# Fewer modulation sums in attention, more in the first feed-forward layer: a two-layer decoder trunk in fp32

## The chip, the cores and the metric

The kernel runs on one core of one Trainium2 chip. The metric is the device time of one execution in microseconds, as the median of the runs shown. Rows of the trace come from one profiled execution.

## The reference

`x` is (1, 256, 1024), all in fp32. Two layers; the first mixes by dilated attention, the second by a gated recurrence, and each is followed by a SwiGLU layer. What matters here is the modulation and the normalisation of q and k:

```python
c_act = jax.nn.silu(c)
for i in range(DEPTH):
    mod = c_act @ ada_w[i] + ada_b[i]          # ada_w[i]: 1024 x 6144
    sh1, sc1, g1, sh2, sc2, g2 = jnp.split(mod[:, None, :], 6, axis=-1)
    h = rms_norm(x, norm_mix[i]) * (1.0 + sc1) + sh1
    ...  # y = dilated_attention(h, ...) or hgrn2_mixer(h, ...)
    x = x + g1 * y
    h = rms_norm(x, norm_ffn[i]) * (1.0 + sc2) + sh2
    x = x + g2 * swiglu(h, ffn_w1[i], ffn_w3[i], ffn_w2[i])

# in dilated_attention, for each of three head groups g (8 heads of 128)
q = rms_norm(qkv[:, :, g, 0], q_gain[g])
k = rms_norm(qkv[:, :, g, 1], k_gain[g])
v = qkv[:, :, g, 2]
```

## The kernel before

**Units.** All weight matrices pass through the core in 126 units of 128 x 2048 numbers. A unit is loaded by a DMA (`raw`), rounded to fp32r by ScalarE (`round_unit`, `whi`), its rest is formed by VectorE (`split_unit`, `wlo`, L1388), and TensorE multiplies high by high, low by high and high by low (L516, 24 products of 512 columns, or 48 of 256). ScalarE and VectorE work two units ahead: in their step m they round and split unit m + 2, and beside it they do what follows from TensorE's unit m. Units 0 to 35 are the q, k, v products of attention, in four pairs of heads with nine units each (`pr, j = divmod(m, 9)`); 36 to 39 are its output product; then come 33 units of the feed-forward layer 0 (`M_FFN0` = 40; unit r of the layer is unit 40 + r, and "unit 18 of the layer" below is r = 18). In the middle of that layer the units repeat in threes: two of them form a block of gate and up products (kinds 0 and 1), the third (kind 2) is a product with w2. After kind 1 ScalarE takes the silu (L1228), VectorE multiplies (L1726), TensorE transposes (L855), and the result is rounded and split (L1718).

**Attention beside the units.** A chunk of q and k (256 x 512) is squared by ScalarE (`qk_square`), reduced by VectorE (`qk_reduce`, L1614), ScalarE takes the root (`qk_rsqrt`, L1012 and L1014), and VectorE refines it and scales the chunk (`qk_normalise`, L1483 to L1488 and two of L1627). TensorE transposes the scaled chunk (`qk_transposes`, L697) behind the next unit. In the pairs from the second on, the reduction lies in steps with j = 1, 3, 5, the normalisation in those with j = 2, 4, 6, and the transposes behind unit j = 3 to 8. There the heads of the pair before are also attended: in even steps TensorE does scores (L716) and values (L742), ScalarE copies the values' bank and VectorE the rest (`att_out`, L1672), VectorE takes the maximum (`att_max`) and, after the exponential, divides (`att_normalise`, L1662 and L1665). In the first pair only the projections run, and the chunks end with units 3, 4 and 5.

**Modulation.** `c_act @ ada_w` is not a product of TensorE: VectorE adds 128 rows of `ada_w` at a time, times a number for each row (`ada_op`, L1409, a "sum" below), to an accumulator `acc`; eight sums make a block of 1024 columns. The two accumulators alternate. GpSimd loads each piece of 512 KB into a ring of two (`ada_load`), the next one when the sum two before is done, and clears the accumulator by a memset (L385) once the sixth of the eight sums of the block before is done, which lets the last load of that block go. When a block is complete, a **task** reduces it over partitions on TensorE (`reduce_task`: L586 for a row of 512 gate values, two tasks a block; L589 for shift and scale), into bank 7, and VectorE copies it out (`ada_evac`, L1463, L1465, L1474). A task waits for its sums, for the evacuation of the task before it, and for `att_out`, if that bank was last used by the values. Tasks stand on TensorE behind the unit that `tasks_at` names in attention, and **before** it in the feed-forward layer; the evacuation stands at the end of VectorE's step of the same number:

```python
# TensorE, feed-forward layer
for task in tasks_at(M_FFN0 + r):
    reduce_task(task)
# VectorE, feed-forward layer: step r
split_unit(base + r + AHEAD)
...
if kind == 1:
    ...  # gated product L1726, waits for ScalarE's silu
for n in range(*ada_in_ffn(f, r)):
    ada_op(n)
...  # ada_evac of the tasks at r
```

Where all this stands is written by hand; there is no scheduler. `ada_done(m)` gives how many pieces are summed up by step m of attention, and `ada_in_ffn` spreads the rest of the first eleven blocks over steps 4 to 28 of the layer.

Of the kernel before, what the change touches and what calls it, by code (L numbers as in the profile page):

```python
# [16 lines left out]
KC = D // P  # L17
# [17 lines left out]
QU = 9  # L35
# [2 lines left out]
ADA_RING = 2  # L38
ADA_BLOCKS = 6 * D // ADA_COLS
ORDER0 = (0, 2, 4, 1, 3, 5, 6, 7, 8)  # L40
ADA_FFN0 = 8 * KC
ADA_FFN1 = 11 * KC
LEVELS = 8
PRODUCTS = LEVELS + 2
# [2 lines left out]
M_FFN0 = M_OUT0 + 4  # L47
# [44 lines left out]
def hybrid_trunk(nc, a, out):  # L92
    TABLE = 2 * P + P - 1
    GH = NG * HEADS
    with ExitStack() as ctx:
# [356 lines left out]
        def qk_last(m):  # L452

            pr, j = divmod(m, QU)
            first = 3 if pr == 0 else 1
            step = 1 if pr == 0 else 2
            n, odd = divmod(j - first, step)
            return 3 * pr + n if pr < PAIRS and odd == 0 and 0 <= n < 3 else None
# [529 lines left out]
        def _(act):  # L988
            count = {}

            def copy(dst, src):
                return nc.scalar.activation(dst, src, ACT.Copy)  # L992

            def round_unit(m):

                if m >= UNITS:
                    return
                act.wait_ge(raw_in[m % RAW], need[m])
                if m >= SPL and m not in spare_hi:
                    act.wait_ge(s["pe_unit"], m - SPL + 1)  # L1000
                copy(hi_of(m), raw[:, m % RAW, :]).then_inc(s["rounded"], 1)
# [150 lines left out]

            def qkv_extra(m):
                pr, j = divmod(m, QU)
                if qk_last(m - 1) is not None:
                    qk_rsqrt(qk_last(m - 1))
                if qk_last(m) is not None:
                    qk_square(qk_last(m))
                if pr >= 1:
                    J = 4 * (pr - 1) + j // 2  # L1160
                    if j % 2 == 0 and j > 0:
                        att_out(J - 1)
                    if j % 2 == 0 and j < 8:
                        att_exp(J)
                    if j % 2 == 1:
                        att_evac(J)
                for n, which in qk_sets(m):
                    qk_evac(n, which)
                if pr < PAIRS and j >= 7:
                    v_evac(pr, j - 7)  # L1170

            gains = cols[:, GAIN0:GAIN0 + 2 * NG]
            act.wait_ge(s["cols_s"], 2)
            for m in range(2, PURE):
                round_unit(m + AHEAD)
                qkv_extra(m)
            def after_tile_0(q, base):
# [201 lines left out]
        def _(dve):  # L1379
# [295 lines left out]
            def qkv_extra(m):  # L1675
                pr, j = divmod(m, QU)
                J = 4 * (pr - 1) + j // 2
                if pr >= 1 and j % 2 == 0 and j > 0:
                    att_out(J - 1)
                if pr >= 1 and j % 2 == 0 and j < 8:  # L1680
                    att_max(J)
                for n in range(ada_done(m - 1), ada_done(m)):
                    ada_op(n)
                if pr >= 1 and j % 2 == 0 and j < 8:
                    att_normalise(J)
                if qk_last(m - 1) is not None:
                    qk_normalise(qk_last(m - 1))
                if qk_last(m) is not None:
                    qk_reduce(qk_last(m))

            for m in range(2, PURE):
                split_unit(m + AHEAD)
                qkv_extra(m)
                for r in tasks_at(m):
                    ada_evac(r)
# [213 lines left out]

def tasks_at(m):  # L1910

    late = {3: [7], 14: [8], 15: [9], 23: [10]}
    return {12: [0], 14: [1], 19: [2], 23: [3], 27: [4], 28: [5], 32: [6]}.get(m, []) + late.get(m - M_FFN0, [])


HGRN_TASK = 11
# [2 lines left out]

def ada_done(m):  # L1920

    return 2 * KC + max(0, m - 5) * 8 // 5


def ada_in_ffn(f, r):
# [42 lines left out]
```

## Time and profile before

| what | value |
|---|---|
| median of 3 runs | 852.75 us (851.1 to 854.27) |
| the profiled execution, its time | 851.16 us |
| the profiled execution, its span | 849.2 us |
| TensorE busy | 820.2 us, 97% |
| VectorE busy | 604.9 us, 71% |
| ScalarE busy | 434.4 us, 51% |
| GpSimd busy | 121.6 us, 14% |
| L1409, the sum | 80 of mean 1279 ns |
| L992, rounding of a unit | mean 1901 ns |
| mean granted clock of TensorE | 0.996 |

The time of an execution holds the span of the trace and some 2 us around it. TensorE is busy nearly throughout. The other engines work beside it, each with its own queue in program order; they cost time only where TensorE waits for them. In the timelines a row is a group of like instructions: its start in us from the start of the span, its duration, and in brackets how long the engine was idle before and what ended that. Rows of one engine can overlap by about 0.1 us, since an instruction starts before the one ahead has written its last result.

### The profile page before, as it was taken

How to read it: one execution, taken by the hardware profiler on the slowest of the kernel's cores; microseconds unless marked ns; L12 is line 12 of the kernel's file. 1: busy time of each engine (PE TensorE's matmuls, PEld its weight loads, DVE VectorE, ACT ScalarE, POOL GpSimd, SP SyncE). 2: the span in 40 equal slices, each digit the busy share in tenths (PEclk: the TensorE clock that was granted, in tenths of full speed). 3: DMA queues.
4: the chain of work that ended last, by engine and by line, in shares of the span. 5: the costliest groups of instructions: out<-in, count | busy, mean ns of one | idle time of the engine just before them, and what ended most of it. 6: DMA issues, size and time to landing. Idle time of an engine off the chain costs nothing.

```text
span 849.2 us, 12126 instructions
## 1 busy us (share of the span) xinstructions
PE 820.2 (97%) x4830; PEld 681.3 (80%) x4830; DVE 604.9 (71%) x745; ACT 434.4 (51%) x553; POOL 121.6 (14%) x154
## 2 busy tenths in 40 slices
PE   4999999999999999999999999989999999999998
PEld 2778888887878988888888888878788888887886
DVE  4897898788888777477656776778688756644544
ACT  5265454454535566344334466786686644334431
POOL 3000111111111100001010000376730000000000
PEclk9899999999999999999999999999999999999999
DMA  9997888887877835588787755544344567765521
GB/s 323 366 355 265 292 261 277 278 249 247 274 260 245 280 108 188 191 283 276 262 289 244 259 163 193 168 129 146 126 159 163 191 200 232 253 215 168 178 100 50
DMA packets 122107, 189.05 MB, mean 223 GB/s; under 512 B 5683, under 2 KB 91048, under 8 KB 122052
## 3 DMA queue, kind: packets, MB, share of 16 engines
q1 hardware_dynamic: 109796, 146.10, 52.9%
q0 software_dynamic: 12256, 42.18, 14.9%
q8 instruction: 38, 0.62, 0.3%
q14 instruction: 17, 0.14, 0.1%
HBM read 187.18 MB, written 1.09 MB: 222 GB/s over the span
## 4 chain that ended last, share of the span: by engine, by line
PE 75%; DVE 9%; POOL 4%; issue 4%; ACT 3%; SPq 2%; DMA 2%; DVEq 0%; ACTq 0%; POOLq 0%
PE bank L516 65%; POOL arena L410 3%; PE bank L716 2%; PE bank L742 2%; POOL arena L409 2%; DVE acc L1409 2%; SPq L309 1%; DMA raw<-in_attn_w_qkv_dram 1%; PE bank L589 1%; PE bank L855 1%; PE bank L697 1%; DMA x<-in_x_dram 1%; PE bank L586 1%; DVE wlo L1388 1%; SPq L300 1%
## 5 line engine op out<-in xcount | busy, mean ns | idle before, releaser
L1388 DVE TENSOR_TENSOR wlo<-raw,whi 128x2048 fp32r<-128x2048 f32 x120 | 275.4, 2299 | 43.3 <-ACT whi L992 43.2
L992 ACT ACTIVATE whi<-raw 128x2048 fp32r<-128x2048 f32 (+1 forms) x124 | 235.5, 1901 | 24.8 <-DMA raw<-in_attn_w_qkv_dram 15.3
L516 PE MATMUL bank<-whi,hT_hi 128*128 128x512 f32 (+1 forms) x728 | 194.5, 391 | 2.0 <-DVE arena L1627 1.2
L516 PE MATMUL bank<-wlo,hT_hi 128*128 128x512 f32 (+1 forms) x752 | 193.4, 381 | 0.0
L516 PE MATMUL bank<-whi,hT_lo 128*128 128x512 f32 (+1 forms) x728 | 187.0, 380 | 0.0
L516 PEld LDWEIGHTS bank<-wlo,hT_hi 128*128 128x128 f32 x752 | 137.4, 188 | 27.6
L516 PEld LDWEIGHTS bank<-whi,hT_lo 128*128 128x128 f32 x728 | 132.7, 188 | 26.1
L516 PEld LDWEIGHTS bank<-whi,hT_hi 128*128 128x128 f32 x728 | 129.6, 188 | 29.6 <-issue 5.4
L393 POOL DMA_DIRECT2D ada_w<-in_ada_w_dram x80 | 42.8, 535 | 509.7 <-DVE acc L1409 492.5
L1409 DVE SCALAR_TENSOR_TENSOR acc<-ada_w,cact,acc 128x1024 f32<-128x1024 f32 x80 | 102.3, 1279 | 5.6 <-DMA ada_w<-in_ada_w_dram 3.5
L1228 ACT ACTIVATE arena<-bank 128x256 f32<-128x256 f32 x44 | 14.5, 381 | 166.8 <-PE bank L516 166.8
L1726 DVE TENSOR_TENSOR arena<-bank,arena 128x256 f32<-128x256 f32 x44 | 16.6, 419 | 112.3 <-ACT arena L1228 112.3
L516 PE MATMUL bank<-whi,oT_hi 128*128 128x512 f32 x240 | 69.2, 404 | 0.0
L516 PE MATMUL bank<-wlo,oT_hi 128*128 128x512 f32 x240 | 65.9, 390 | 0.0
L516 PE MATMUL bank<-whi,oT_lo 128*128 128x512 f32 x240 | 65.8, 390 | 0.0
L516 PEld LDWEIGHTS bank<-wlo,oT_hi 128*128 128x128 f32 x240 | 45.1, 188 | 9.8
L516 PEld LDWEIGHTS bank<-whi,oT_lo 128*128 128x128 f32 x240 | 45.1, 188 | 9.6
L992 ACT ACTIVATE oT_hi<-bank 128x512 fp32r<-128x512 f32 (+1 forms) x38 | 17.6, 464 | 62.6 <-PE bank L742 43.2
L516 PEld LDWEIGHTS bank<-whi,oT_hi 128*128 128x128 f32 x240 | 43.2, 188 | 7.9 <-issue 0.5
L992 ACT ACTIVATE arena<-bank 128x512 f32<-128x512 f32 (+3 forms) x63 | 29.8, 530 | 12.1 <-PE bank L725 7.0
L1135 ACT ACTIVATE arena<-arena,small 128x768 f32<-128x768 f32 (+1 forms) x16 | 12.5, 779 | 34.4 <-DVE small L1649 23.9
L409 POOL TENSOR_TENSOR arena<-arena 128x512 f32<-128x512 f32 x7 | 11.2, 1599 | 76.0 <-DVE arena L1768 69.5
(181 smaller groups left out, 809.7 us busy)
## 6 DMA issues: line engine op xcount, KB each, us to landing
raw<-in_ffn_w_dram SPq DMA_DIRECT2D x88, 512.0 KB, 4.9
ada_w<-in_ada_w_dram POOLq DMA_DIRECT2D x80, 512.0 KB, 4.9
raw<-in_attn_w_qkv_dram SPq DMA_DIRECT2D x62, 512.0 KB, 6.2
raw<-in_ffn_w_dram SPq DMA_DIRECT2D x22, 1024.0 KB, 5.0
raw<-in_hgrn_w_in_dram SPq DMA_DIRECT2D x16, 1024.0 KB, 5.4
arena<-in_ada_w_dram SPq DMA_DIRECT2D x16, 512.0 KB, 9.8
raw<-in_attn_w_qkv_dram SPq DMA_DIRECT2D x4, 1024.0 KB, 5.8
raw<-in_attn_w_out_dram SPq DMA_DIRECT2D x4, 1024.0 KB, 6.6
```

What stands on the lines that cost most here:

```text
L393: pool.dma_start(ada_w[:, n % ADA_RING], a["ada_w"][layer, k * P:(k + 1) * P, b * ADA_COLS:(b + 1) * ADA_COLS]).then_inc(ada_in[n % ADA_RI ...
L409: pool.tensor_tensor(v(E)[:, :, 0, :], mid, v(Gk)[:, :, 0, :], ALU.subtract)
L410: i = pool.tensor_tensor(v(E)[:, :, 1, :], v(G)[:, :, 1, :], mid, ALU.subtract)
L516: mm = nc.tensor.matmul(dst[t][c][:, 0:n], lhs[:, k0 + k, t * P:(t + 1) * P], w[:, k, c * 512:c * 512 + n], start=start and k == 0, stop=s ...
L716: mm = nc.tensor.matmul(dst, qT[:, pr % 2, g, base + qt * P:base + (qt + 1) * P], kT[:, pr % 2, g, base:base + w], start=True, stop=True)
L742: mm = nc.tensor.matmul(out_bank(J), vN[:, pr % 2, kt, c:c + P], probs(J)[1][:, i * P:(i + 1) * P], start=i == 0, stop=i == len(todo) - 1)
L992: return nc.scalar.activation(dst, src, ACT.Copy)
L1135: nc.scalar.activation(pr_, pr_, ACT.Exp, bias=stat(J, 2), accum_out=stat(J, 3)).then_inc(s["att_p"], 1)
L1228: i = nc.scalar.activation(sil[:, t], gate_bank(j, t)[:, 0:FC], ACT.Silu)
L1388: nc.vector.tensor_tensor(wlo[:, m % RAW, :], raw[:, m % RAW, :], fp(hi_of(m)), ALU.subtract).then_inc(s["split"], 1)
L1409: nc.vector.scalar_tensor_tensor(out=acc[:, blk % 2], in0=ada_w[:, n % ADA_RING], scalar=cact[:, k:k + 1], in1=acc[:, blk % 2], op0=ALU.mu ...
L1726: i = nc.vector.tensor_tensor(hid[:, t], gate_bank(j, t)[:, FC:2 * FC], sil[:, t], ALU.mult)
```

## The change

Eight pieces move from attention to the feed-forward layer 0: `ada_done` gives 4 sums in three steps instead of 8 in five, and `ADA_FFN0` starts the rest eight earlier. The tasks are moved accordingly. In a step of attention only the first sum stays ahead of `att_normalise` and `qk_normalise`, and the second goes behind them. In the first pair the root on ScalarE goes ahead of the rounding, and the normalisation on VectorE ahead of the split of the same step.

```diff
-ADA_FFN0 = 8 * KC
+ADA_FFN0 = 7 * KC
...
             def qkv_extra(m):
                 pr, j = divmod(m, QU)
-                if qk_last(m - 1) is not None:
+                if pr and qk_last(m - 1) is not None:
                     qk_rsqrt(qk_last(m - 1))
...
             for m in range(2, PURE):
+                if m < QU and qk_last(m - 1) is not None:
+                    qk_rsqrt(qk_last(m - 1))
                 round_unit(m + AHEAD)
                 qkv_extra(m)
...
-                for n in range(ada_done(m - 1), ada_done(m)):
+                sums = range(ada_done(m - 1), ada_done(m))
+                for n in sums[:1]:
                     ada_op(n)
                 if pr >= 1 and j % 2 == 0 and j < 8:
                     att_normalise(J)
-                if qk_last(m - 1) is not None:
+                if pr and qk_last(m - 1) is not None:
                     qk_normalise(qk_last(m - 1))
+                for n in sums[1:]:
+                    ada_op(n)
                 if qk_last(m) is not None:
                     qk_reduce(qk_last(m))
 
             for m in range(2, PURE):
+                if m < QU and qk_last(m - 1) is not None:
+                    qk_normalise(qk_last(m - 1))
                 split_unit(m + AHEAD)
                 qkv_extra(m)
...
-    late = {3: [7], 14: [8], 15: [9], 23: [10]}
-    return {12: [0], 14: [1], 19: [2], 23: [3], 27: [4], 28: [5], 32: [6]}.get(m, []) + late.get(m - M_FFN0, [])
+    late = {3: [6], 12: [7], 18: [8], 19: [9], 25: [10]}
+    return {12: [0], 14: [1], 19: [2], 25: [3], 30: [4], 31: [5]}.get(m, []) + late.get(m - M_FFN0, [])
...
-    return 2 * KC + max(0, m - 5) * 8 // 5
+    return 2 * KC + max(0, m - 5) * 4 // 3
```

The changed kernel's lines lie two further down from L1388 on, and seven further from L1718 on.

VectorE, first pair, from the reduction of the second chunk on (L1388 split, L1614 reduction, L1483 to L1627 normalisation). Before:

```order
L1614 TENSOR_REDUCE small<-sq 128x8
L1388 TENSOR_TENSOR wlo<-raw,whi 128x2048
L1483 TENSOR_SCALAR small<-small 128x8
L1484 TENSOR_TENSOR small<-small 128x8
L1486 TENSOR_TENSOR small<-small 128x8
L1488 SCALAR_TENSOR_TENSOR small<-small 128x8
L1627 TENSOR_TENSOR arena<-bank,small 128x512 x2
```

and after:

```order
L1616 TENSOR_REDUCE small<-sq 128x8
L1485 TENSOR_SCALAR small<-small 128x8
L1486 TENSOR_TENSOR small<-small 128x8
L1488 TENSOR_TENSOR small<-small 128x8
L1490 SCALAR_TENSOR_TENSOR small<-small 128x8
L1629 TENSOR_TENSOR arena<-bank,small 128x512 x2
L1390 TENSOR_TENSOR wlo<-raw,whi 128x2048
```

The split of unit 7 moves from ahead of the normalisation to behind it.

VectorE, feed-forward layer 0, around the copy of task 8's row (L1726 gated product, L1409 sum, L1463 copy of the gate, L1718 rest of the hidden block). Before, in steps 14 and 15:

```order
L1388 TENSOR_TENSOR wlo<-raw,whi 128x2048
L1409 SCALAR_TENSOR_TENSOR acc<-ada_w,cact,acc 128x1024
L1463 COPY gate<-bank 128x512
L1388 TENSOR_TENSOR wlo<-raw,whi 128x2048
L1726 TENSOR_TENSOR arena<-bank,arena 128x256 x2
L1409 SCALAR_TENSOR_TENSOR acc<-ada_w,cact,acc 128x1024
L1463 COPY gate<-bank 128x512
```

and after, in steps 18 and 19:

```order
L1390 TENSOR_TENSOR wlo<-raw,whi 128x2048
L1733 TENSOR_TENSOR arena<-bank,arena 128x256 x2
L1411 SCALAR_TENSOR_TENSOR acc<-ada_w,cact,acc 128x1024 x2
L1465 COPY gate<-bank 128x512
L1390 TENSOR_TENSOR wlo<-raw,whi 128x2048
L1725 TENSOR_TENSOR oT_lo<-bank,oT_hi 128x512
L1411 SCALAR_TENSOR_TENSOR acc<-ada_w,cact,acc 128x1024
L1465 COPY gate<-bank 128x512
```

The first of the two copies stood behind a split and one sum; now it stands behind a gated product and two sums.

TensorE at the same place (L586 is a task's reduction; products with `hT` are of kinds 0 and 1, with `oT` of kind 2). Before, tasks 8 and 9 and what follows:

```order
L586 MATMUL bank<-acc,ones 128x512
L516 MATMUL bank<-whi,hT_hi 128x512 x4
L516 MATMUL bank<-wlo,hT_hi 128x512 x4
L516 MATMUL bank<-whi,hT_lo 128x512 x4
L516 MATMUL bank<-whi,hT_hi 128x512 x4
L516 MATMUL bank<-wlo,hT_hi 128x512 x4
L516 MATMUL bank<-whi,hT_lo 128x512 x4
L586 MATMUL bank<-acc,ones 128x512
L516 MATMUL bank<-whi,hT_hi 128x512 x4
```

and after:

```order
L586 MATMUL bank<-acc,ones 128x512
L516 MATMUL bank<-whi,hT_hi 128x512 x4
L516 MATMUL bank<-wlo,hT_hi 128x512 x4
L516 MATMUL bank<-whi,hT_lo 128x512 x4
L516 MATMUL bank<-whi,hT_hi 128x512 x4
L516 MATMUL bank<-wlo,hT_hi 128x512 x4
L516 MATMUL bank<-whi,hT_lo 128x512 x4
L586 MATMUL bank<-acc,ones 128x512
L516 MATMUL bank<-whi,oT_hi 128x512 x4
```

The two tasks have one unit between them as before; that unit was of kind 0 and is now of kind 1.

## Rows read from the trace of the kernel before

**Rows 1.** Waits of TensorE: what waited <- for what: us, times, longest.
```profile
PE bank L697 <- DVE arena L1627: 4.5, 5, 1.7
```

**Rows 2.** Timeline, TensorE, attention: start, duration, engine, line, product; idle before.
```profile
65.58 1.18 PE L516 MATMUL bank<-whi,hT_hi 128*128 128x512 f32 x4 [1.25 <-DVE arena L1627]
...
192.51 0.66 PE L697 MATMUL bank<-ident,arena 128*128 128x128 f32 x4 [0.52 <-DVE arena L1627]
...
209.96 0.65 PE L697 MATMUL bank<-ident,arena 128*128 128x128 f32 x4 [1.29 <-DVE arena L1627]
...
247.06 0.66 PE L697 MATMUL bank<-ident,arena 128*128 128x128 f32 x4 [1.67 <-DVE arena L1627]
```

**Rows 3.** Timeline, VectorE, attention.
```profile
109.47 2.28 DVE L1388 TENSOR_TENSOR wlo<-raw,whi 128x2048 fp32r<-128x2048 f32 x1
...
187.19 2.66 DVE L1409 SCALAR_TENSOR_TENSOR acc<-ada_w,cact,acc 128x1024 f32<-128x1024 f32 x2
...
190.50 0.17 DVE L1483 TENSOR_SCALAR small<-small 128x8 f32<-128x8 f32 x1
...
206.79 1.39 DVE L1483 TENSOR_SCALAR small<-small 128x8 f32<-128x8 f32 x1
...
255.49 0.29 DVE L1672 TENSOR_TENSOR oT_lo<-bank,oT_hi 128x128 fp32r<-128x128 f32 x1 [0.38 <-ACT oT_hi L992]
```

**Rows 4.** Timeline, GpSimd, the memset of an accumulator.
```profile
207.17 0.98 POOL L385 MEMSET acc<- 128x1024 f32 x1
```

**Rows 5.** Timeline, VectorE, first pair.
```profile
56.17 2.28 DVE L1388 TENSOR_TENSOR wlo<-raw,whi 128x2048 fp32r<-128x2048 f32 x1
58.37 0.17 DVE L1483 TENSOR_SCALAR small<-small 128x8 f32<-128x8 f32 x1
...
60.24 1.21 DVE L1614 TENSOR_REDUCE small<-sq 128x8 f32<-128x1024 f32 x1
...
64.23 1.29 DVE L1627 TENSOR_TENSOR arena<-bank,small 128x512 f32<-128x512 f32 x2
```

**Rows 6.** Timeline, TensorE, tasks and unit starts in attention.
```profile
110.71 1.02 PE L586 MATMUL bank<-acc,ones 128*128 128x512 f32 x2
...
255.34 1.17 PE L516 MATMUL bank<-whi,hT_hi 128*128 128x512 f32 x4
```

**Rows 7.** Timeline, ScalarE, first pair: the root.
```profile
56.29 0.30 ACT L1012 ACTIVATE small<-small,eps 128x8 f32<-128x8 f32 x1 [0.44 <-DVE small L1614]
56.62 0.21 ACT L1014 ACTIVATE small<-small 128x8 f32<-128x8 f32 x1
```

**Rows 8.** Timeline, TensorE, feed-forward layer 0, start of unit 19.
```profile
429.01 1.07 PE L516 MATMUL bank<-whi,oT_hi 128*128 128x512 f32 x4
```

**Rows 9.** Timeline, VectorE, feed-forward layer 0.
```profile
414.97 0.68 DVE L1463 COPY gate<-bank 128x512 f32<-128x512 f32 x1
...
429.90 0.76 DVE L1726 TENSOR_TENSOR arena<-bank,arena 128x256 f32<-128x256 f32 x2 [4.65 <-ACT arena L1228]
430.57 1.27 DVE L1409 SCALAR_TENSOR_TENSOR acc<-ada_w,cact,acc 128x1024 f32<-128x1024 f32 x1
```

**Rows 10.** Stretches of TensorE: length, busy (x instructions), granted clock, DMA share, GB/s.
```profile
23.50:24.00 0.50, 0.50 (x1) 0.53 1.10 350
...
30.20:30.40 0.20, 0.20 (x2) 0.60 1.06 364
140.00:320.00 180.00, 175.40 (x995) 1.00 0.76 244
```

**Rows 11.** Timeline, TensorE, the start.
```profile
10.08 0.39 PE L610 MATMUL bank<-ident,rows 79*128 79x79 f32 x1 [7.66 <-DMA rows<-in_ada_b_dram]
10.27 3.43 PE L604 MATMUL bank<-x,ident 128*128 128x512 f32 x4
...
14.41 1.02 PE L604 MATMUL bank<-x,ident 128*128 128x512 f32 x2
...
21.01 1.95 PE L597 MATMUL bank<-ones,acc 128*128 128x1 f32 x16
```

## Prediction, written before the changed kernel ran

> **What bounds the kernel now.** I read the table of waits first, TensorE's part. After the start, the only waits of TensorE in attention are for line 1627, the VectorE product that writes a normalised chunk: 4.5 us in five waits at the transposes (L697) [rows 1]; one more, of 1.25 us, is at a matrix product (L516) [rows 2]. TensorE is busy 97% of the span, so a microsecond that it waits is a microsecond of the result, and work on the other engines is free until it makes TensorE wait. The timeline of TensorE gives the places [rows 2]: 1.25 us before unit 6, then 0.52 us at 192.51 (two more like it, 0.51 and 0.52 us, at 141.28 and 177.33), 1.29 us at 209.96 and 1.67 us at 247.06. By the order of the code these five are the transposes in units 16, 21, 23, 25 and 30, after VectorE's steps 15, 20, 22, 24 and 29: exactly the steps of the last three pairs that have both a normalisation and two sums. In the feed-forward layer the table shows no wait of TensorE for VectorE. So attention can give back at most 5.7 us, and anything that VectorE is given in the feed-forward layer must stay off TensorE's path.
>
> **Part 1: fewer sums in attention.** The new formula gives 1, 1, 2 sums a step where it gave 1 or 2 (eight in five steps). Steps 15, 22 and 24 now have one; steps 11, 20 and 29 have two, but only the first is ahead of the normalisation. A pair of sums takes 2.66 us [rows 3], one 1.27 [rows 9], and what stands behind a single sum starts 1.2 us after the sum's start, since their ends overlap. So at each of the five places the chunk is ready 1.2 us earlier. Three waits of 0.5 become a margin of 0.7. The wait of 1.29 nearly goes (0.09 left). The one of 1.67 would leave 0.47, if nothing else changed.
>
> Something else does change. In the last two cases a short instruction of the normalisation, L1483, took 1.39 us instead of 0.17 [rows 3], and on GpSimd a memset of the accumulator lies from 207.17 to 208.15 [rows 4], where L1483 ends (208.18). It comes 0.82 us after the end of the sum that lets it go. That sum is the 14th, 22nd, 30th, 38th, 46th of the count. Before, the 30th and 38th lay in steps 24 and 29, directly ahead of a normalisation. Now the 14th, 38th and 46th are followed by a split of weights, the 30th by a reduction, and only the 22nd (step 22) by a normalisation. So both delays go, and with them what was left of the two waits; one new delay comes at step 22. There the single sum ends at about 188.4, the memset would end at 190.3, then comes the rest of the normalisation, 1.87 [rows 5] less the 0.17 of L1483, and so the chunk is ready at 192.0, as TensorE arrives (192.51 less 0.52 is 191.99): 0.1 left, bounds 0 and 0.5. Sum of this part: -4.5 + 0.1 = **-4.4 us**.
> The Trainium skill (SBUF — State Buffer, "SBUF: two separate sides") says that VectorE and GpSimd share one pair of ports as an exclusive lock, and that the instruction that starts first keeps it. The long L1483 agrees with a lock, but not with the order, since it is recorded 0.38 us ahead of the memset; by the strict rule step 22 would not be held up and the sum would be 0.1 lower.
>
> **Part 2: the second sum behind the chunk.** It matters where the reduction of the accumulator on TensorE needs that very sum. Task 0 (unit 12) needs eight sums, and the eighth is now the second one of step 11. It can start when the last L1627 is done, at 109.47 [rows 3], and ends at 110.75; TensorE would start the reduction at 110.71 [rows 6]. With 0.05 to react, +0.1 us. Task 4 moves to unit 30 and needs the 32nd sum, the second of step 29. Chunk ready there at 247.0 - 2.4 = 244.6, sum done at 245.8, TensorE at the reduction at 245.39 + 0.4 = 245.8: another +0.1. Task 5 moves to unit 31, which has an even position in its pair: there TensorE has just written the attention output to bank 7, which the reduction wants, so it must wait until VectorE has read it (L1672). At the like place TensorE goes on at 255.34 and L1672 runs from 255.49 to 255.78 [rows 3, 6]: **+0.5 us**. Before, no task stood in such a unit. The other moves (3 to unit 25, 6 to the feed-forward layer) find their sums and evacuations done. Sum: +0.7.
>
> **Part 3: first pair, normalisation ahead of the splits.** Unit 6 waits for the second normalisation. Before, VectorE did from 56.17 on: split (2.2), normalise (1.87), reduce (1.13), split (2.2), normalise, ready at 65.52 [rows 5]. Now two things come off and two on: the second split is behind, and each normalisation waits for its root on ScalarE, which the split covered. The root is two short instructions, 56.29 to 56.83 [rows 7], about 0.75 us from reduction to use. So 56.17 + 0.75 + 1.87 + 2.2 + 1.13 + 0.75 + 1.87 + 0.1 = 64.84 to 64.9: **-0.6 us**. ScalarE rounds unit 6 after the first root, 56.83 to 58.75, just as VectorE comes to split it, so nothing is lost there. TensorE arrives at 64.33, so -1.2 is the bound; 0 if the rounding slips.
>
> **Part 4: eight chunks in the feed-forward layer.** 32 sums in 25 steps, 24 before. VectorE idles 4.65 us ahead of each gated product [rows 9], so the 8 x 1.2 us and their transfers are hidden: nothing. But the tasks move too. Tasks 8 and 9 stood before units 14 and 15 and now stand before units 18 and 19. Task 9 may start only when VectorE has copied task 8's result out (one bank for both). In step 14 VectorE does that in the middle of a unit. Step 18 is the second half of a gate product: there VectorE first waits for the unit to end and for ScalarE's silu, then makes the gated product, then **two** sums (step 18 is one of the seven with two), and only then the copy. TensorE stands meanwhile, because the task is the next thing in its queue. On the clock of the trace of before: unit 18 is over and unit 19 starts at 429.01 [rows 8]; the product starts at 429.90 and the sum at 430.57, each sum takes 1.2 until the next starts, so the copy starts at 432.97; it takes 0.68 like the one at 414.97 [rows 9]; 433.65, and 0.05 to react: 433.70 - 429.01 = **+4.7 us**. It was never paid before, as task 9's predecessor was copied 2 us early. Tasks 7 and 10 have no such neighbour.
>
> **Part 5: the clock after that pause.** Since the start TensorE has had no pause above 1.67 us, and the clock stayed granted at 1.00 [rows 2, 10]. It fell once, at 23.5 us: from 19.2 on TensorE had run two sets of 16 products of one column each and begun one wide product [rows 11]. It stayed at 0.50 (1.2 GHz, against 2.4) until 30.4 [rows 10]. Likewise, after a wait of 7.66 us at the start, four wide products took 3.43 us, while two took 1.02 later [rows 11]. Bounds of the price: 0 (no fall) and 3.4 us (6.8 us at half speed, all under work). I take 1.5, near the start's rows: 3.43 - 2 x 1.02 = 1.4. A pause of 4.6 us is a longer lull than the one that brought the clock down, so I count it in: **+1.5 us**.
> The Trainium skill (TensorE: Matmul & The Clock Gate, "HAM oscillation — how this bites in real kernels") says that pauses between bursts bring the engine back to half clock each time. By that rule the 1.5 belongs in the sum, 854.7; without it the sum is 853.2.
>
> **Sum.** -4.4 + 0.7 - 0.6 + 4.7 + 1.5 = +1.9 us. The profiled execution took 851.16 for a span of 849.2; it lies 1.6 below the median of 852.75. I put the sum on the median: 854.7.
>
> **Rivals.**
> - The clock holds through the pause: +0.4, 853.2. For it: it held through every pause up to 1.67. Against: the fall at 23.5 followed a lighter lull.
> - The clock stays at half for the whole 6.8 us under work: +3.8, 856.6; above 7.7 us it would pass 857.0. For it: that is what the one recorded fall did. Against: part of that time would lie in the pause.
> - Slower than before: the waits in attention come back. The margin gained at the three places is 0.7 and at the other two about the same; a disturbance of the size of the memset's 1.2 us exceeds it by 0.5. If the memsets or the sum's own transfer fall ahead of the normalisation at all five places, 5 x 0.5 = 2.6 us return: 857.3. It decides from 0.7 us of delay on. Against: GpSimd follows the count of sums, and by the count only step 22 is hit.
> - The change does what it says and no more: the pause in the feed-forward layer does not arise, because the copy is done before TensorE wants the bank. Then -4.3: 848.4. Against: the order of the code on both engines leaves no way around it; unit 19's task is queued behind it.
>
> **How the numbers follow.** Forecast 0.58, clock holds 0.22, clock long at half 0.10, waits come back 0.06, no pause 0.04. The runs of before spread by 1.6 around their median, so 851.5 to 857.0 takes the first three cases. About 0.5% (4.3 us: below 848.5, above 857.0) is what a measurement here can tell from no change. Faster 0.03 (most of the last case), slower 0.08 (most of the fourth case and the tail of the third), the rest the same.
>
> **What would show it.** In the profile of the changed kernel: no wait of L697 above 0.2 us for the normalised chunk; a wait of about 0.6 us before unit 6; a wait of 0.5 us of L586 for L1672's like near 253; one wait of 4.5 us of L586 for VectorE's copy of the gate near 428, with product, two sums and the copy under it; the granted clock at 0.50 for some microseconds behind it, and matrix products at twice their spacing. The forecast is wrong if that wait is missing or under 3 us, or if the five waits in attention are still there.

## The result, and the profile after

| | before | after |
|---|---|---|
| median | 852.72 us (20 runs, 850.97 to 854.95) | 854.14 us (20 runs, 852.75 to 855.95) |
| ratio to before, 95% interval | | 1.0016 [1.0008, 1.0023] |
| profiled execution: time, span | 851.16, 849.2 us | 854.91, 853.0 us |
| TensorE busy | 820.2 us | 826.1 us |
| mean granted clock of TensorE | 0.996 | 0.989 |

The change makes the kernel 1.4 us slower, which is less than the 0.5% that counts as a difference here, and the forecast of 854.7 lies 0.6 us beside it.

The table of waits after the change, TensorE's part (what waited <- for what: us, times, longest). The five waits of L697 and the one of L516 [rows 1, 2] are gone from it; L1411 is the sum, L1674 reads the attention output:

```profile
PE bank L586 <- DVE acc L1411: 5.0, 2, 4.8
...
PE bank L586 <- DVE oT_lo L1674: 0.3, 1, 0.3
```

Where these lie on TensorE, in its timeline after the change. The first row is the start of unit 6 and the second the transposes of unit 23; they answer to [rows 2]. Then come tasks 4 and 5, and task 9 with the end of unit 18 ahead of it ([rows 8]) and two groups behind it:

```profile
65.64 1.19 PE L516 MATMUL bank<-whi,hT_hi 128*128 128x512 f32 x4
...
190.91 0.66 PE L697 MATMUL bank<-ident,arena 128*128 128x128 f32 x4
...
241.24 1.13 PE L586 MATMUL bank<-acc,ones 128*128 128x512 f32 x2 [0.22 <-DVE acc L1411]
...
250.59 1.10 PE L586 MATMUL bank<-acc,ones 128*128 128x512 f32 x2 [0.35 <-DVE oT_lo L1674]
...
423.30 1.07 PE L516 MATMUL bank<-whi,hT_lo 128*128 128x512 f32 x4
429.13 2.04 PE L586 MATMUL bank<-acc,ones 128*128 128x512 f32 x2 [4.77 <-DVE acc L1411]
430.19 2.69 PE L516 MATMUL bank<-whi,oT_hi 128*128 128x512 f32 x4
...
435.60 0.60 PE L855 MATMUL bank<-ident,arena 128*128 128x128 f32 x4
```

VectorE under the long wait, after the change; it answers to [rows 9]. Gated product, both sums, then the copy, and TensorE goes on 0.1 us after the copy's end:

```profile
425.09 0.76 DVE L1733 TENSOR_TENSOR arena<-bank,arena 128x256 f32<-128x256 f32 x2 [5.70 <-ACT arena L1230]
425.76 2.67 DVE L1411 SCALAR_TENSOR_TENSOR acc<-ada_w,cact,acc 128x1024 f32<-128x1024 f32 x2
428.35 0.68 DVE L1465 COPY gate<-bank 128x512 f32<-128x512 f32 x1
```

TensorE's granted clock behind it, in stretches of 2 us (columns as in [rows 10]). Half speed, 1.2 GHz against 2.4, from 428 to 435, all of it but the first microsecond under work:

```profile
428.00:430.00 2.00, 0.87 (x1) 0.55 1.09 338
430.00:432.00 2.00, 2.00 (x5) 0.50 0.86 277
432.00:434.00 2.00, 2.00 (x7) 0.50 0.25 102
434.00:436.00 2.00, 2.00 (x11) 0.74 0.00 0
```

### The profile page after: what moved, and what is told of

It is laid out like the page before. It is cut to its first block, busy times and chain, and to the rows that moved or that the text cites. A ratio compares the mean times of both kernels' runs of the same rounds, so it can differ in the third digit from the quotient of the medians.

```text
span 853.0 us, 12126 instructions
## 1 busy us (share of the span) xinstructions
PE 826.1 (97%) x4830; PEld 685.2 (80%) x4830; DVE 604.1 (71%) x745; ACT 433.6 (51%) x553; POOL 121.4 (14%) x154
## 4 chain that ended last, share of the span: by engine, by line
PE 81%; DVE 8%; POOL 5%; issue 3%; ACT 3%; DMA 1%; POOLq 0%; ACTq 0%; DVEq 0%
PE bank L516 67%; POOL arena L410 3%; PE bank L636 2%; PE bank L716 2%; PE bank L742 2%; POOL arena L409 2%; PE bank L589 1%; PE bank L855 1%; PE bank L586 1%; PE bank L697 1%; DVE wlo L1390 1%; PE bank L725 1%; DVE acc L1411 1%; PE bank L553 1%; PE bank L604 1%
## 5 line engine op out<-in xcount | busy, mean ns | idle before, releaser
L516 PE MATMUL bank<-whi,hT_hi 128*128 128x512 f32 (+1 forms) x728 | 194.3, 390 | 0.9 <-ACT hT_hi L992 0.8
L516 PE MATMUL bank<-wlo,hT_hi 128*128 128x512 f32 (+1 forms) x752 | 193.4, 381 | 0.0
L516 PE MATMUL bank<-whi,hT_lo 128*128 128x512 f32 (+1 forms) x728 | 187.1, 381 | 0.0
L516 PEld LDWEIGHTS bank<-wlo,hT_hi 128*128 128x128 f32 x752 | 137.4, 188 | 27.7
L516 PEld LDWEIGHTS bank<-whi,hT_lo 128*128 128x128 f32 x728 | 132.7, 188 | 26.1
L516 PEld LDWEIGHTS bank<-whi,hT_hi 128*128 128x128 f32 x728 | 129.7, 188 | 28.2 <-issue 4.9
L1411 DVE SCALAR_TENSOR_TENSOR acc<-ada_w,cact,acc 128x1024 f32<-128x1024 f32 x80 | 102.3, 1278 | 14.2 <-DMA ada_w<-in_ada_w_dram 13.1
L516 PE MATMUL bank<-whi,oT_hi 128*128 128x512 f32 x240 | 71.0, 412 | 0.0
L516 PE MATMUL bank<-wlo,oT_hi 128*128 128x512 f32 x240 | 66.8, 394 | 0.0
L516 PE MATMUL bank<-whi,oT_lo 128*128 128x512 f32 x240 | 66.1, 391 | 0.0
L516 PEld LDWEIGHTS bank<-wlo,oT_hi 128*128 128x128 f32 x240 | 45.6, 190 | 10.0
L516 PEld LDWEIGHTS bank<-whi,oT_lo 128*128 128x128 f32 x240 | 45.4, 189 | 9.8
L516 PEld LDWEIGHTS bank<-whi,oT_hi 128*128 128x128 f32 x240 | 43.7, 191 | 8.9 <-issue 1.5
L1674 DVE TENSOR_TENSOR oT_lo<-bank,oT_hi 128x128 fp32r<-128x128 f32 x16 | 4.6, 290 | 23.7 <-ACT oT_hi L992 23.7
```

The costliest lines, as they stand in the source:

```text
L516: mm = nc.tensor.matmul(dst[t][c][:, 0:n], lhs[:, k0 + k, t * P:(t + 1) * P], w[:, k, c * 512:c * 512 + n], start=start and k == 0, stop=s ...
L1411: nc.vector.scalar_tensor_tensor(out=acc[:, blk % 2], in0=ada_w[:, n % ADA_RING], scalar=cact[:, k:k + 1], in1=acc[:, blk % 2], op0=ALU.mu ...
```

## Experiments on the feed-forward layer

What the later task costs, and whether the half clock has a price of its own. Edits are against the changed kernel.

**Tasks 8 and 9 one unit earlier.**

```diff
-    late = {3: [6], 12: [7], 18: [8], 19: [9], 25: [10]}
+    late = {3: [6], 12: [7], 17: [8], 18: [9], 25: [10]}
```

> The changed kernel with tasks 8 and 9 of the feed-forward layer one unit earlier, before units 17 and 18, so that the copy of task 8 stands in a step without a gated product. Main theory (a pause of 4.9 us, and behind it the clock at half, 1.3 to 2.9 us): no wait of L586 above 0.5 us in this layer, the clock falls only at the start, and the time is 846.3 to 847.9, which is 5 to 6 us under the kernel before. Rival (the clock's fall costs nothing of its own, since the start's phase decides): 849.2. Rival (the pause is not the copy's place in the queue but the bank or the sums themselves): the wait stays and the time is 854.

Measured: 848.04 us (847.47 to 848.37), ratio 0.994 [0.9924, 0.9956]. The pause and the fall of the clock behind it are gone: by the ratios 6.5 us. It stopped just short of the range expected (846.3 to 847.9), since task 8 now waits for its last sum, which the expectation had left out. TensorE's timeline:

```profile
412.63 1.12 PE L586 MATMUL bank<-acc,ones 128*128 128x512 f32 x2 [0.81 <-DVE acc L1411]
```

**The copy ahead of both sums in step 18.** Same work, another order in VectorE's queue.

```diff
-                    for n in range(*ada_in_ffn(f, r)):
+                    early = f == 0 and r == 18
+                    sums = range(*ada_in_ffn(f, r))
+                    for n in sums[:0] if early else sums:
                         ada_op(n)
...
+                    for n in sums[0:] if early else ():
+                        ada_op(n)
```

> The changed kernel with the copy of task 8 ahead of the two sums of step 18, nothing else. Main theory: the pause is gated product plus copy, 4.9 - 2.4 = 2.5 us. If the clock holds through a pause of 2.5 us, the time is 854.1 - 2.4 - (1.3 to 2.9), that is 848.8 to 850.4; if it falls all the same, 851.7. Rival (sums are not in the pause): 854.

Measured: 850.27 us (848.5 to 851.89), ratio 0.997 [0.996, 0.9981].

**The copy between the two sums** (`sums[:1]` and `sums[1:]` in the same lines).

> The changed kernel with the copy of task 8 between the two sums of step 18. Main theory: a pause of 3.7 us. With the clock falling behind it: 852.9; with the clock holding: 850.0 to 851.6. Beside the run with the copy ahead of both sums it shows from what length of pause the clock is lost.

Measured: 851.45 us (850.0 to 853.11), ratio 0.9981 [0.9968, 0.9993].

TensorE's timeline at task 9, first with the copy ahead of both sums, then with the copy between them:

```profile
427.34 1.10 PE L586 MATMUL bank<-acc,ones 128*128 128x512 f32 x2 [2.18 <-issue]
```

```profile
427.82 2.04 PE L586 MATMUL bank<-acc,ones 128*128 128x512 f32 x2 [3.38 <-DVE acc L1411]
```

The wait falls from 4.77 to 3.38 and 2.18 us, 1.3 for each sum taken out of the way. So the wait is what stands in VectorE's queue ahead of the copy, and the label "acc L1411" names a sum where the copy behind it was meant. Even behind 2.18 us of idleness the clock fell in the profiled execution, for 3.4 us (a stretch of 1 us there, copy ahead of both sums):

```profile
430.00:431.00 1.00, 1.00 (x4) 0.50 0.74 138
```

Both times lie where the expectations put a clock that holds (848.8 to 850.4 and 850.0 to 851.6), and yet the traces show a fall. It was a shorter one than either branch had: 3.4 us at half in each, against 6.8 in the changed kernel. Counted as work at half speed (an estimate) that is about 1.3 us of time less, with the shorter waits 3.9 and 2.7 us in all, and the ratios give 3.9 and 3.0. Nor does the clock fall behind such a wait every time. A mean clock of 0.996 is what the kernel before has with 6.8 us at half at the start and nothing else, and no execution of any kernel has more. Two of the 12 executions with the copy ahead of both sums and three of the 12 with it between them are at 0.996, so there, by this reckoning, the clock held.

**The pause filled with work.** Five fp32 products of 512 columns (ten matmuls in the trace) ahead of task 9, into a bank that is free, their result unused: the pause stays, but TensorE works in it.

```diff
+                        if r == 19:
+                            pe.wait_ge(s["f_lo"], hidden_after(r))
+                            for _ in range(5):
+                                nc.tensor.matmul(bank[6][:], ident[:], x[:, 0, 0:512], start=True, stop=True)
```

> The changed kernel with five fp32 products of 512 columns on TensorE, into the free bank 6, put ahead of task 9, where TensorE would stand idle; their result is not used. They take about 4.3 of the 4.9 us. Main theory (the clock's fall has a price of its own): the clock stays at 1.00 there, the way from unit 18 to unit 19 stays 4.9 us plus the task, and the time is 854.1 - (1.3 to 2.9) = 851.2 to 852.8. Rival (no price of its own): 854.1. Rival (the fill reaches past the copy and adds to the pause): above 854.5.

Measured: 852.01 us (851.0 to 852.77), ratio 0.9991 [0.998, 1.0002], 2.1 us below the changed kernel. TensorE's timeline, and a stretch behind the pause:

```profile
423.63 4.45 PE L807 MATMUL bank<-x,ident 128*128 128x512 f32 x10
428.56 1.10 PE L586 MATMUL bank<-acc,ones 128*128 128x512 f32 x2 [0.48 <-issue]
...
432.26 0.60 PE L859 MATMUL bank<-ident,arena 128*128 128x128 f32 x4
```

```profile
430.00:432.00 2.00, 2.00 (x10) 1.00 0.68 240
```

Unit 18's last group starts at 423.30 after the change, and a group starts each 0.91, so the pause is 429.13 - 424.21 = 4.92 us; here, where the first filling product starts in unit 19's place, it is 428.56 - 423.63 = 4.93. The same pause, but the clock stays at 1.00. From the task to the next transposes it takes 3.70 us here and 6.47 in the changed kernel: 2.8 us in these two executions, 2.1 by the ratios. That is the price of the half clock alone.

The Trainium skill (TensorE: Matmul & The Clock Gate, "HAM oscillation — how this bites in real kernels") says that pauses between bursts bring the engine back to half clock each time. By that rule the fall was to be expected, and at this place the trace agrees. That it comes each time isn't what the runs with the shorter waits show: by the mean clock, five of the 24 executions there held it.

## Experiments on attention

Which part of the change removed the six waits? Edits are against the kernel before, unless said.

**The first pair's part alone.**

```diff
-                if qk_last(m - 1) is not None:
+                if pr and qk_last(m - 1) is not None:
...
             for m in range(2, PURE):
+                if m < QU and qk_last(m - 1) is not None:
+                    qk_normalise(qk_last(m - 1))
                 split_unit(m + AHEAD)
```

and the same for `qk_rsqrt` on ScalarE.

> The kernel before with the first pair's part of the change alone (root ahead of the rounding, normalisation ahead of the split in the first nine steps). Main theory: unit 6 waits 0.4 to 0.9 us instead of 1.25, the rest is untouched, and the time is 0.6 to 0.8 us under the kernel before (852.6): 851.8 to 852.0. Rival (TensorE arrives at unit 6 later or earlier with the start's phase, and the part gains nothing of its own): 852.6.

Measured: 852.7 us (850.44 to 855.25) against 853.5 for before on that chip, ratio 0.9992 [0.9979, 1.0006]: 0.7 us less by the ratio, inside the noise. The wait of L516 is gone and the five of L697 stay.

**The second sum behind the chunk, alone.** Here my theory fell.

```diff
-                for n in range(ada_done(m - 1), ada_done(m)):
+                sums = range(ada_done(m - 1), ada_done(m))
+                for n in sums[:1]:
                     ada_op(n)
...
+                for n in sums[1:]:
+                    ada_op(n)
                 if qk_last(m) is not None:
```

> The kernel before with the order of the sums alone: the second sum of a step goes behind the normalised chunk; no chunk and no task is moved. Main theory (the five waits in attention are the second sum ahead of the chunk, and the memset behind that sum): all five go, since with the sum its memset falls behind the chunk too, and the time is 852.6 - 4.5 = 848.1. Rival (VectorE has too much to do in these steps and needs the eight chunks gone): the sums behind push the splits and the next step's start, at least 1.5 us of waits stay, and the time is 849.6 or more.

Measured: 856.71 us (856.22 to 857.38), ratio 1.0041 [1.0026, 1.0056], slower than both kernels. The five waits are gone, as the main theory had it, but longer ones stand elsewhere; the rival's number came out (849.6 or more), though not by its mechanism, as the run that puts the sum late only in some steps shows. VectorE's waits for the pieces of `ada_w` come to 18.5 us here, the longest 5.3, where the kernel before has 3.5 in five and the changed one 13.1 in nine, longest 3.1. The line of the table of waits, and the place of the longest in VectorE's timeline (steps 29 and 30):

```profile
DVE acc L1409 <- DMA ada_w<-in_ada_w_dram: 18.5, 10, 5.3
```

```profile
243.02 1.28 DVE L1409 SCALAR_TENSOR_TENSOR acc<-ada_w,cact,acc 128x1024 f32<-128x1024 f32 x1
...
246.41 1.28 DVE L1409 SCALAR_TENSOR_TENSOR acc<-ada_w,cact,acc 128x1024 f32<-128x1024 f32 x1
252.94 1.28 DVE L1409 SCALAR_TENSOR_TENSOR acc<-ada_w,cact,acc 128x1024 f32<-128x1024 f32 x1 [5.25 <-DMA ada_w<-in_ada_w_dram]
```

GpSimd issues the load that the last of these waits for, and SyncE a unit of 1 MB, in this order; then the same two in the kernel before:

```profile
243.72 0.37 SPq L309 DMA_DIRECT2D raw<-in_attn_w_out_dram  x1
```

```profile
244.59 0.53 POOL L393 DMA_DIRECT2D ada_w<-in_ada_w_dram  x1 [3.07 <-DVE acc L1409]
```

```profile
243.75 0.53 POOL L393 DMA_DIRECT2D ada_w<-in_ada_w_dram  x1 [0.86 <-DVE acc L1409]
```

```profile
245.09 0.37 SPq L309 DMA_DIRECT2D raw<-in_attn_w_out_dram  x1
```

The ring has two places. The second sum, put off by the 2.4 us of the chunk's work, frees its place 0.8 us later, and the load that refills it goes out at 244.59, behind the unit's transfer (itself 1.4 us earlier here) instead of ahead of it, while the DMA engines are full from 246 to 254. It lands 8.3 us after its issue. Step 30 has two sums as well, the second waits for that load, and `att_normalise` and the chunk of step 31 stand behind it in VectorE's queue. TensorE's wait, and its clock after it:

```profile
260.93 1.54 PE L725 MATMUL bank<-ident,arena 128*128 128x128 f32 x6 [3.15 <-DVE arena L1665]
```

```profile
262.00:264.00 2.00, 1.67 (x9) 0.50 0.69 258
...
268.00:270.00 2.00, 2.00 (x6) 0.50 0.81 256
```

**Both parts, with the sums and tasks as before.**

> The kernel before with both parts of the order, the first pair's and the second sum behind the chunk; no chunk and no task moved. Main theory: the gains add, 852.6 - 4.5 - 0.7 = 847.4, under every kernel so far, and TensorE has no pause in the feed-forward layer. Rival (the chunks must move): 849 or more.

Measured: 855.52 us (852.85 to 859.36), ratio 1.0026 [1.001, 1.0041]. The same wait at the same place (2.98 us at 260.94), the same fall of the clock. A second miss, from the same cause.

**Late only where no pair follows.** This tells the ring apart from the late sum as such: steps 9, 14, 19, 24 and 29, which another step with two sums follows, keep both sums ahead. The edit is against the run with the second sum behind the chunk, alone.

```diff
-                for n in sums[:1]:
+                ahead = 2 if ada_done(m + 1) - ada_done(m) == 2 else 1
+                for n in sums[:ahead]:
...
-                for n in sums[1:]:
+                for n in sums[ahead:]:
```

> The kernel before with the second sum behind the normalised chunk only in those steps whose next step has a single sum (in steps 12, 15, 20, 22 and so on; not in 9, 14, 19, 24 and 29, which another pair follows). Theory (what made the order alone slower is the ring of two: a late second sum issues its follow-up load late, and a pair in the next step then waits in VectorE's queue for that transfer, 3.2 and 5.3 us): with no pair behind a late sum the long waits of VectorE for ada_w go (none above 2 us in attention), there is no wait of L725 above 0.3 us, the waits of L697 of 0.5 us in units 16, 21 and 23 go, those of 1.3 and 1.7 stay: 852.7 - 1.5 = 851.2, bounds 850.7 and 851.7. Rival (a late second sum is itself what costs, whatever follows): long waits for ada_w stay, and the time is at or above that of before, 852.7 or more.

Measured: 849.59 us (849.28 to 849.78, 5 runs), ratio 0.9956 [0.9942, 0.997]. The waits are as the theory of the ring has them, the three of 0.5 gone and the longest for `ada_w` 1.9:

```profile
PE bank L697 <- DVE arena L1627: 3.0, 2, 1.7
```

```profile
DVE acc L1409 <- DMA ada_w<-in_ada_w_dram: 5.3, 6, 1.9
```

But the time fell by more than the 1.5 expected, 3.7 by the ratio. Part of it is that a wait costs more than its listed idle time. The transposes of unit 16, where the wait was 0.51, with the row ahead of them; first the kernel before, then this one:

```profile
140.28 0.49 PE L725 MATMUL bank<-ident,arena 128*128 128x128 f32 x3
141.28 0.66 PE L697 MATMUL bank<-ident,arena 128*128 128x128 f32 x4 [0.51 <-DVE arena L1627]
141.69 1.19 PE L516 MATMUL bank<-whi,hT_hi 128*128 128x256 f32 x8
```

```profile
140.21 0.49 PE L725 MATMUL bank<-ident,arena 128*128 128x128 f32 x3
140.54 0.60 PE L697 MATMUL bank<-ident,arena 128*128 128x128 f32 x4
140.89 1.19 PE L516 MATMUL bank<-whi,hT_hi 128*128 128x256 f32 x8
```

From L725 to the next unit 1.41 us and 0.68: the wait of 0.51 costs 0.73, since without it the groups overlap by 0.16 and the transposes are shorter. Three of them are 2.2 us. The rest of the 3.7 goes at least in part to the clock, which differs between executions of one kernel: the five runs have 0.994 in the median, the executions of before on their chip 0.991. At a like clock the gap is smaller. The kernel before has 28 executions on all chips with a mean clock of 0.993 or 0.994, and their median is 851.9; the five here, four of them at these values, have 849.6, so 2.3 us less.

**The memset one sum later.** GpSimd waits for one more sum before it clears an accumulator of attention.

```diff
+                        if blk < 8:
+                            pool.wait_ge(s["ada_used"], n - 2 * KC - ADA_RING + 1)
                     pool.memset(acc[:, blk % 2], 0.0).then_inc(s["ada_zero"], 1)
```

> The kernel before, with the memset of the accumulators of attention held until one sum later (GpSimd waits for one more sum), nothing else. If the memset is what makes the short instruction of the normalisation long (1.39 us where it takes 0.17), both long ones in steps 24 and 29 go, or move behind the chunk; the waits of TensorE of 1.29 and 1.67 us fall to about 0.1 and 0.5, those of 0.5 stay, and the time falls by 1.9 us: a median of 851.0 against 852.9. Rival, the short instruction is slow for another reason (its place behind a pair of sums): the waits stay, 852.9; or the memset falls on another instruction ahead of a chunk and the time is the same.

Measured: 849.69 us (848.68 to 854.2), ratio 0.9976 [0.9961, 0.9991], 2.1 us less. TensorE's waits for the chunk, VectorE's short instruction in step 24, and the memset, which now lies behind the chunk:

```profile
PE bank L699 <- DVE arena L1629: 2.1, 4, 0.5
```

```profile
207.04 0.16 DVE L1485 TENSOR_SCALAR small<-small 128x8 f32<-128x8 f32 x1
```

```profile
212.51 0.95 POOL L387 MEMSET acc<- 128x1024 f32 x1 [5.10 <-DVE acc L1411]
```

The instruction took 1.39 us before [rows 3]. So the memset made it long. This is the cheapest edit of all: two lines gain 2.1 us, where the whole change loses 1.4.

## A version that beats both

**The changed kernel with tasks 4, 5 and 9 at other units.** Task 5 leaves the even unit, and 4 and 9 get a unit or two more.

```diff
-    late = {3: [6], 12: [7], 18: [8], 19: [9], 25: [10]}
-    return {12: [0], 14: [1], 19: [2], 25: [3], 30: [4], 31: [5]}.get(m, []) + late.get(m - M_FFN0, [])
+    late = {3: [6], 12: [7], 18: [8], 20: [9], 25: [10]}
+    return {12: [0], 14: [1], 19: [2], 25: [3], 32: [4], 34: [5]}.get(m, []) + late.get(m - M_FFN0, [])
```

> The changed kernel with four tasks elsewhere: 4 and 5 behind units 32 and 34 (where no new sum or attention output is waited for), 8 and 9 before units 18 and 20. Main theory (every new wait of the change is a task's place): the waits of 0.22, 0.35 and 4.8 us of L586 go, the one of 0.8 us that the places 17 and 18 brought does not come, and the time is 848.0 - 0.8 - 0.6 = 846.6 to 847.0. If instead moving the chunks costs something of its own in the feed-forward layer (their transfers, VectorE later), it stays at 848 or above.

Measured: **845.6 us** (845.15 to 847.18), ratio **0.9914 [0.9898, 0.993]**, 0.9% faster than before, and 1 us below the range expected. (Of the four tasks that the expectation names, task 8 keeps the place that the change gave it.) In its table of waits TensorE waits for neither a chunk nor a sum; the longest behind the start are the recurrence's for VectorE, 0.6 each:

```profile
PE bank L891 <- DVE arena L1790: 3.4, 7, 0.6
```

The next two runs are on another chip, whose kernel before is 1.35 us faster in the median (852.15 against 853.5), so differences of medians and of ratios are both given.

**This version with both sums ahead again** (`for n in sums:` and nothing behind).

> The best version so far (tasks 4, 5 and 9 at other units, 845.6 us) with the second sum ahead of the normalised chunk again, everything else kept. Theory A (fewer sums and late second sum each give what they cost): steps 11, 20 and 29 have two sums with a normalisation behind them; a pair delays the chunk by 1.2 us, and with a margin of 0.7 each costs 0.5 us of TensorE at the transposes (units 12, 21 and 30): 845.6 + 1.5 = 847.1, bounds 846.6 and 848.5 (the memset at step 29 if it falls ahead of the chunk). Theory B (the late second sum costs as much as it gives, since its follow-up load is late and the next sum waits for its DMA): the waits of VectorE for ada_w fall from about 13 us back toward 4, and the time stays at 845.0 to 846.2.

Measured: 847.49 us (847.38 to 848.7), ratio 0.9947 [0.9932, 0.9962].

```profile
PE bank L697 <- DVE arena L1629: 1.9, 3, 0.8
```

Three waits come back in units 12, 21 and 30, and time with them: 1.9 us between the medians, 2.8 by the ratios. The waits for `ada_w` stay as they were (13.4 us in ten, 13.7 in nine). With fewer pairs, none next to another, the late sum does what it should.

**This version with the first pair as before.**

> The best version so far (845.6 us) with the first pair as before (root behind the rounding, normalisation behind the split). If the first pair's part gives what was predicted (0.6 us; the trace of the changed kernel showed 0.8): 846.2 to 846.4, and the wait ahead of unit 6 goes from about 0.4 back to 1.25. Rival: the part gives nothing that lasts, 845.6.

Measured: 846.47 us (845.82 to 847.36), ratio 0.9933 [0.9919, 0.9948], 0.9 us more between the medians and 1.6 by the ratios, whose intervals still overlap. The trace shows it at the place itself. TensorE at the start of unit 6:

```profile
66.60 1.23 PE L516 MATMUL bank<-whi,hT_hi 128*128 128x512 f32 x4 [0.93 <-DVE arena L1627]
```

From the transposes ahead of unit 6 to unit 6 it is 1.97 us here and 1.17 in the best version, 0.8 us apart, with the clock at half for 10.2 us at the start of both.

## Why the prediction was right

- **Part 1, -4.4, and Part 2, +0.7: right in the sum, both sizes off.** From the start of unit 6 to the group of 18 score products near the end of attention (287.53 before, 281.87 after) the two profiled executions differ by 5.7 us, of which 1.7 is task 6, which moved out; so 4.0 less, where -4.4 + 0.7 is 3.7. But each wait costs 0.2 more than the table lists (shown at unit 16), so the five waits of 4.5 us were worth 5.6. The new ones were worth more too: task 4 waits 0.22 and task 5 0.35, about 1.0 together with the 0.2 of each; the small lags at task 0 and in step 22 come to some 0.2 and 0.3 where 0.1 each stood. Two errors of about 1 us cancelled, which is luck.
- **The memset and the short instruction: right.** The delay moved to step 22, as counted. VectorE's and GpSimd's timelines after the change (the kernel with the late memset shows the cause):

```profile
187.92 1.20 DVE L1485 TENSOR_SCALAR small<-small 128x8 f32<-128x8 f32 x1
```

```profile
187.57 0.55 POOL L393 DMA_DIRECT2D ada_w<-in_ada_w_dram  x1 [6.70 <-DVE acc L1411]
188.12 0.97 POOL L385 MEMSET acc<- 128x1024 f32 x1
```

  The instruction is again recorded ahead of the memset, by 0.2 us, and ends with it; so does the one behind it (L1486, 1.13 us where 0.16 is usual), so the records don't tell which of the two is held. That a lock of the ports is what holds it is the Trainium skill's rule (SBUF — State Buffer, "SBUF: two separate sides"); the runs show that the memset is the cause and don't show through what.
- **Part 3, -0.6: right in sign and about in size.** The clearest figure is 0.8 us at the place itself (the best version against the same with the first pair as before, with like starts). The run of the part alone gives 0.7 by the ratio, within noise. The wait of about 0.6 that was to stay ahead of unit 6 isn't in the profile after the change: the clock was at half at the start for 10.2 us there instead of 6.8, and TensorE reached unit 6 1.2 us later (65.50, not 64.33). With the short start of the filled-pause run a wait of 0.81 stays.
- **Part 4, +4.7: right, 4.92 measured**, by the mechanism named, down to the order of product, two sums and copy. It was this one place that turned a gain into a loss.
- **Part 5, +1.5: right that it falls, low in size.** The filled pause gives 2.1 (about 1 either way by the intervals), the two traces 2.8. The term was sized by the start's four wide products, taken to run at half clock. The profile of the kernel before has the granted clock at 1.00 in that stretch, so it doesn't show that their length was the clock's:

```profile
10.50:13.50 3.00, 3.00 (x4) 1.00 1.06 351
```

  The fall behind the pause lasted 6.8 us, and 5.9 of them were under work (429.13 to 435.0).
- **The sum.** With the measured sizes, -4.0 - 0.8 + 4.9 + 2.1 = +2.2; the medians differ by 1.4 (0.7 to 2.0 by the interval). The 0.8 left is within the uncertainty of the clock's term. Between the two profiled executions it closes better: the spans differ by 3.8 us, and 0.1 up to unit 6, -5.7 to the scores, +1.7 for task 6, +4.9 and +2.8 make 3.8.
- **Of the rivals**, the long stay at half clock is what the profiled execution did, 6.8 us of it, at 2.8 us of time where the rival had 3.4; the forecast was nearer in time, since attention and the first pair gave back 0.5 more than their terms and the clock costs 2.1 by the ratios. By the time alone the rival in which the clock holds (853.2) would be hardly worse than the forecast; the trace and the filled pause rule it out. "The waits come back" had the right worry and the wrong place: what can bring a late chunk back isn't a memset but a piece that isn't there yet, and the prediction didn't price that. It looked at what moves a sum, not at what the moved sum lets go. By itself that part costs 3.5 us by the ratio (2.2 to 4.8) instead of giving any. It works in the change because eight pieces left attention at the same time, so that no step with two sums follows another: the run that puts the sum late only where no pair follows shows that this condition is enough.

## What to carry to other kernels

When a consumer is moved later in its queue, follow what it frees: with a ring of two its refill is late as well, falls behind other transfers, and stalls whatever stands behind the next user. When work is moved to a stage with slack, list who is queued behind it there and who waits for them; here the moved sums brought TensorE no wait that the tasks' places couldn't take away, and the place of one reduction cost 7 us, pause and clock together, which changing a number gave back. Price a pause of TensorE with the half clock behind it, and a listed wait with about 0.2 us on top.

## What the runs showed of the hardware

- TensorE's clock fell after idle times of 2.2, 3.0, 3.2, 3.4 and 4.8 us, for 3.4 to 10.2 us, in the profiled executions; it didn't after 1.7 [rows 2]. The longest stays at half followed the waits in attention, not the longest idle time.
- It also fell where TensorE had hardly been idle but had run products of one column. In the run of the first pair's part alone it was at half for 3.4 us from 195.4 on, behind a wait of 0.52 and 16 such products, which the kernel before has in the same place at 1.00. So a stretch without long waits isn't proof of the full clock.

```profile
192.60 0.66 PE L697 MATMUL bank<-ident,arena 128*128 128x128 f32 x4 [0.52 <-DVE arena L1629]
193.09 1.84 PE L589 MATMUL bank<-ones,acc 128*128 128x1 f32 x16
```

```profile
195.50:198.50 3.00, 3.00 (x9) 0.50 0.95 282
```

- The executions of one kernel differ by 4 us, and the clock has a part in it: of the kernel before, the 9 with a mean clock of 0.996 have a median of 851.4, the 18 with 0.989 or 0.990 one of 854.4. At the start it was at half for 7 us in some executions and 10 in others; 3.4 us more at half are up to 1.7 us of time (an estimate, at half speed). The stretch after 31 us, the kernel before and then the changed one:

```profile
31.00:31.50 0.50, 0.50 (x3) 1.00 1.11 352
```

```profile
31.00:31.50 0.50, 0.50 (x3) 0.50 1.11 350
```

- In seven of the profiled executions it also fell for 3.4 us where the recurrence begins (between 526 and 541), again right behind 16 products of one column and an idle time of 0.35 us; in the other seven it stayed at 1.00 behind the same products. Where it did, TensorE's waits for VectorE in the recurrence were 3.4 to 4.2 us, elsewhere 4.8 to 5.1: part of such a fall seems to be hidden in waits that TensorE would have had anyway.
